# First two gate and up pairs, and the second feed-forward's entry unit, with both parts of x in one matmul

## The reference, cut to what matters

```python
x = x + rms_norm(mix, norm_mix_post[l])
h2 = rms_norm(x, norm_ffn_pre[l])
ff = jnp.einsum('bsf,fd->bsd',
                jax.nn.silu(jnp.einsum('bsd,df->bsf', h2, w_gate[l]))
                * jnp.einsum('bsd,df->bsf', h2, w_up[l]), w_down[l])
...
# second block: h = rms_norm(x); relu(h @ w_ff1) ** 2 @ w_ff2; 4096 hidden channels
```

## Time and profile before

| what | value |
|---|---|
| median of three runs | 805.6 us |
| span of the profiled execution | 804.3 us |
| PE busy | 798.1 us, 99%, 5838 matmuls |
| PEld busy | 700.9 us, 87% |
| DVE busy | 570.7 us, 71% |
| ACT busy | 465.5 us, 58% |
| POOL busy | 108.7 us, 14% |
| weight loads by SP | 49.8% of 16 DMA engines' span |

### The profile page before, as it was taken

One profiled execution on the slowest core, in us unless ns is written; L12 is line 12 of the kernel. 1 busy time (PEld: TensorE's weight loads), 2 busy tenths in 40 slices (PEclk: granted clock), 3 DMA queues, 4 the chain that ended last, 5 costly groups with the idle time before them and its releaser, 6 DMA issues.

```text
span 804.3 us, 13652 instructions
## 1 busy us (share of the span) xinstructions
PE 798.1 (99%) x5838; PEld 700.9 (87%) x5838; DVE 570.7 (71%) x712; ACT 465.5 (58%) x614; POOL 108.7 (14%) x82
## 2 busy tenths in 40 slices
PE   9999999999999999999999999999999999999998
PEld 7999988788888898888888889987899888888886
DVE  5877996897576586766676688598978865556653
ACT  6679774665534575454454575477787644444442
POOL 0102790662000000000000010111610100000000
PEclk9999999999999999999999999999999999999999
DMA  9844444443653655554655555465323555555641
GB/s 312 296 168 158 159 158 158 152 165 113 214 169 146 222 189 172 206 187 180 210 174 192 208 167 203 165 211 167 129 90 109 202 179 187 209 173 194 202 165 52
DMA packets 37820, 143.03 MB, mean 178 GB/s; under 512 B 9426, under 2 KB 11490, under 8 KB 24320
## 3 DMA queue, kind: packets, MB, share of 16 engines
q1 hardware_dynamic: 36576, 138.69, 49.8%
q0 software_dynamic: 1040, 3.43, 1.2%
q10 hardware_dynamic: 144, 0.04, 0.0%
HBM read 141.08 MB, written 1.06 MB: 177 GB/s over the span
## 4 chain that ended last, share of the span: by engine, by line
PE 93%; DMA 3%; DVE 2%; ACT 1%; issue 0%; POOL 0%; SPq 0%; POOLq 0%
PE ps L2380 8%; PE ps L2373 7%; PE ps L2025 6%; PE ps L2274 6%; PE ps L2272 6%; PE ps L2273 6%; PE ps L1957 6%; PE ps L2031 6%; PE ps L2028 6%; PE ps L1958 6%; PE ps L1959 6%; PE ps L2378 4%; PE ps L2375 4%; PE ps L2133 2%; DMA raw<-w 1%; DMA x<-xT 1%
## 5 line engine op out<-in xcount | busy, mean ns | idle before, releaser
L1178 DVE TENSOR_TENSOR wlo<-raw,whi 128x2048 fp32r<-128x2048 f32 (+2 forms) x128 | 289.4, 2263 | 73.9 <-ACT whi L622 72.5
L622 ACT ACTIVATE whi<-raw 128x2048 fp32r<-128x2048 f32 (+2 forms) x128 | 241.3, 1887 | 105.7 <-DMA raw<-w 105.6
L1957 PE MATMUL ps<-xx,whi 128*128 128x256 f32 x396 | 114.2, 288 | 0.0
L1958 PE MATMUL ps<-xx,whi 128*128 128x256 f32 x396 | 112.0, 283 | 0.0
L1959 PE MATMUL ps<-xx,wlo 128*128 128x256 f32 x396 | 112.0, 283 | 0.0
L2272 PE MATMUL ps<-whi,xx 128*128 128x512 f32 x216 | 84.1, 389 | 0.0
L2273 PE MATMUL ps<-whi,xx 128*128 128x512 f32 x216 | 84.0, 389 | 0.0
L2274 PE MATMUL ps<-wlo,xx 128*128 128x512 f32 x216 | 84.0, 389 | 0.0
L2025 PE MATMUL ps<-whi,xx 128*128 128x512 f32 x208 | 83.0, 399 | 0.0
L2031 PE MATMUL ps<-wlo,xx 128*128 128x512 f32 x208 | 81.1, 390 | 0.0
L2028 PE MATMUL ps<-whi,xx 128*128 128x512 f32 x208 | 81.0, 390 | 0.0
(11 more groups left out here) (322 smaller groups left out, 1366.7 us busy)
## 6 DMA issues: line engine op xcount, KB each, us to landing
raw<-w SPq DMA_DIRECT2D x105, 1024.0 KB, 4.8
raw<-w SPq DMA_DIRECT2D x42, 512.0 KB, 4.8
raw<-w SPq DMA_DIRECT2D x8, 256.0 KB, 6.3
x<-xT SPq DMA_DIRECT2D x4, 256.0 KB, 5.7
work<-bias_scratch POOLq DMA_DIRECT2D x1, 1024.0 KB, 7.2
raw<-w SPq DMA_DIRECT2D x4, 192.0 KB, 3.2
out<-x SPq DMA_DIRECT2D x3, 256.0 KB, 2.5
raw<-w SPq DMA_DIRECT2D x3, 240.0 KB, 3.3
```

What stands on the lines that cost most here:

```text
L622: A(hi, full, ACT.Copy).then_inc(sem("hi_ready"), 1)
L1178: V.tensor_tensor(lo, full, hi.bitcast(F32), ALU.subtract)\
L1957: mm(out, hi, xh[:, tile, :], start=start, stop=False, skip_group_check=skip)
L1958: mm(out, hi, xl[:, tile, :], start=False, stop=False, skip_group_check=skip)
```

## The change

- Pairs 0 and 1 of the first feed-forward and the entry pair of the second go to the wide form. Their banks are `ENTRY_BANKS`: unit 43 in 6 and 1, unit 44 in 0 and 2, gate 1 in 3 and 4, up 1 in 1 and 7; unit 99 in 5 and 6.
- `first_wide` replaces `first_unit` for units 43 and 99. Its first pair of input tiles stays at 256 columns; for the other three the high weight meets `xx` in one matmul, which comes after the wait for `act_lo`.
- `wide_tiles` gets a hook `low`, used by unit 44 to wait for its low weights behind the first 8 matmuls.
- ACT's order gets the low copies of units 43 and 44 ahead of the splits of units 46 and 47, and of the later entry units; the ReLU of the second entry pair goes.
- DVE's order is written anew: `gate_added(0)`, the split of 46, one add of up 0, `norm_factors`, the other add, the split of 47, and only then the wait for `bcs`.
- PE waits for `ple_copy` ahead of gate 1 (it was ahead of down 0), for `bcs` copied inside up 1, and for `gate_r` 2 ahead of down 0.

```diff
-WIDE1 = range(2, PAIRS1)
-WIDE2 = range(1, PAIRS2)
+WIDE1 = range(PAIRS1)
+WIDE2 = range(PAIRS2)
 GATE_BANKS, UP_BANKS = (0, 1), (2, 7)
+ENTRY_BANKS = ((6, 1), (0, 2), (3, 4), (1, 7))
...
             # ACT
+            low_copy(U_F1, 0, lows[0])
+            low_copy(U_F1, 1, lows[0])
             split_hi(U_F1 + RING)
+            low_copy(U_F1 + 1, 0, lows[1])
+            low_copy(U_F1 + 1, 1, lows[1])
             split_hi(U_F1 + 1 + RING)
             bc_copy("n3")
             silu_pair(0)
             hidden_hi(0, "hid", 0, 0)
...
-            relu_pair(0, U_F2, 5)
+            low_copy(U_F2, 0, lows[0])
+            low_copy(U_F2, 1, lows[0])
...
             # DVE
+            gate_added(0, U_F1)
+            split_lo(U_F1 + RING)
+            up_added(U_F1 + 1, 0)
             norm_factors("n3", 1)
-            split_lo(U_F1 + RING)
+            up_added(U_F1 + 1, 1)
+            split_lo(U_F1 + 1 + RING)
             dve.wait_ge(sem("norm_bcs"), before("bcs", "n3") + 1)
-            gate_scaled(0, U_F1, U_F1 % RING)
-            split_lo(U_F1 + 1 + RING)
-            hidden(0, 0, U_F1 + 1, (U_F1 + 1) % RING)
+            gate_scaled()
+            silu_scaled(0)
+            hidden_wide(0, 0)
             hidden_lo(0, 0, "hid", 0)
             for j in range(1, PAIRS1):
+                gate_added(j, u)
+                gate_scaled()
                 split_lo(u + RING)
+                silu_scaled(j)
+                up_added(u + 1, 0)
                 if j < PAIRS1 - 1:
                     split_lo(u + 1 + RING)
+                up_added(u + 1, 1)
+                hidden_wide(j, j % 2)
...
-            relu_square(0, 0, 5)
+            square_wide(0, U_F2, 0)
             hidden_lo(0, 0, "hid2", 8)
...
             # PE
+            def first_wide(u, base, x_name):
+                arrived(u)
+                o = [ps[b] for b in WIDE[u][1]]
+                for pair in range(4):
+                    blocks = [(m, k) for k in (2 * pair, 2 * pair + 1) for m in range(2)]
+                    w = lambda m, k: slice((8 * m + k) * P, (8 * m + k + 1) * P)
+                    pe.wait_ge(sem("act_hi"), before("hi", x_name) + pair + 1)
+                    for m, k in blocks:
+                        mm(o[m][:, 0:T], wlo[:, u % SLOTS, w(m, k)], xh[:, base + k, :], start=k == 0, ...)
+                        if pair == 0:
+                            mm(o[m][:, 0:T], whi[:, u % SLOTS, w(m, k)], xh[:, base + k, :], ...)
+                    pe.wait_ge(sem("act_lo"), before("lo", x_name) + pair + 1)
+                    for m, k in blocks:
+                        high = whi[:, u % SLOTS, w(m, k)]
+                        if pair == 0:
+                            mm(o[m][:, T:2 * T], high, xl[:, base + k, :], ...)
+                            continue
+                        last = mm(o[m][:, :], high, xx[:, base + k, :, :], ...)
...
-            first_unit(U_F1, 8, "n3")
-            first_parts(U_F1 + 1, 8)
+            first_wide(U_F1, 8, "n3")
+            pe.wait_ge(sem("hi_ready"), U_F1 + 2)
+            used(wide_tiles(U_F1 + 1, 8, low=lambda: arrived(U_F1 + 1)))
             norm_stats("n3", sq3)
...
                 first = j == 1
                 pe.wait_ge(sem("lo_ready"), u + 1)
+                if first:
+                    pe.wait_ge(sem("ple_copy"), PLE_EARLY // 2)
+                else:
                     pe.wait_ge(sem("gate_r"), j)
                     pe.wait_ge(sem("hid_y"), j)
+                used(wide_tiles(u, 8, between=(lambda: norm_bc("n3")) if first else None))
                 pe.wait_ge(sem("lo_ready"), u + 2)
+                if first:
                     pe.wait_ge(sem("gate_r"), 1)
+                used(wide_tiles(u + 1, 8, between=factors_read if first else None))
                 pe.wait_ge(sem("lo_ready"), u + 3)
                 pe.wait_ge(sem("hid_lo"), j)
                 if first:
-                    pe.wait_ge(sem("ple_copy"), PLE_EARLY // 2)
+                    pe.wait_ge(sem("gate_r"), 2)
...
-            first_unit(U_F2, 0, "n6", 5)
+            first_wide(U_F2, 0, "n6")
```

More of the change, by code:

```diff
@@ L160, with gate_unit @@
 TURNED = dict(mo=(1, 2, 0, 7), ff=(3, 7, 0, 4))
+def gate_unit(j):
+    return U_F1 + 3 * j - 1 if j else U_F1
 def wide_units():
@@ L167, in wide_units @@
     for j in WIDE1:
-        units += [(U_F1 + 3 * j - 1, GATE_BANKS), (U_F1 + 3 * j, UP_BANKS)]
+        u = gate_unit(j)
+        gate, up = ENTRY_BANKS[2 * j:2 * j + 2] if j < 2 else (GATE_BANKS, UP_BANKS)
+        units += [(u, gate), (u + 1, up)]
     for j in WIDE2:
-        units.append((U_F2 + 2 * j - 1, (UP_BANKS, GATE_BANKS)[j % 2]))
+        units.append((U_F2 + 2 * j - 1, (UP_BANKS, GATE_BANKS)[j % 2]) if j else (U_F2, (5, 6)))
     return {u: (i, banks) for i, (u, banks) in enumerate(units)}
@@ L876, in _ @@
             for j in range(1, PAIRS1):
[L877 to L880, removed]
+                u = gate_unit(j)
+                low_copy(u, 0, lows[0])
                 split_hi(u + RING)
-                if wide:
-                    low_copy(u, 1, lows[0])
-                    low_copy(u + 1, 0, lows[1])
+                low_copy(u, 1, lows[0])
+                low_copy(u + 1, 0, lows[1])
                 silu_pair(j)
@@ L887, in _ @@
                     split_hi(u + 1 + RING)
-                if wide:
-                    low_copy(u + 1, 1, lows[1])
+                low_copy(u + 1, 1, lows[1])
                 hidden_hi(j, "hid", 2 * (j % 2), j % 2)
@@ L1504, in _ @@
             ahead(U_PLE)
[L1507 to L1524, removed]
             def low_added(u, m, out, low):
@@ L1530, in low_added, with gate_added, gate_scaled, silu_scaled @@
                 return V.tensor_tensor(out[:, m, :], ps[banks[m]][:, 0:T], low[:, m, :], ALU.add)
-            def gate_wide(j, u):
-                dve.wait_ge(sem("gated"), j)
+            def gate_added(j, u):
+                if j:
+                    dve.wait_ge(sem("gated"), j)
                 count(low_added(u, 0, two(silu), lows[0]))
                 link(low_added(u, 1, two(silu), lows[0]))
+            def gate_scaled():
                 V.tensor_tensor(two(silu), two(silu), factors_by_tile(2), ALU.mult).then_inc(sem("gate_r"), 1)
-            def up_wide(j, u, m):
-                if m == 0:
-                    dve.wait_ge(sem("silu"), j + 1)
+            def silu_scaled(j):
+                dve.wait_ge(sem("silu"), j + 1)
+                if j:
                     dve.wait_ge(sem("hid_y"), j)
-                    V.tensor_tensor(two(gated), two(silu), factors_by_tile(2), ALU.mult).then_inc(sem("gated"), 1)
+                V.tensor_tensor(two(gated), two(silu), factors_by_tile(2), ALU.mult).then_inc(sem("gated"), 1)
+            def up_added(u, m):
                 count(low_added(u, m, lows[1], lows[1]))
@@ L1550, in hidden_wide @@
                 dve.wait_ge(sem("dve_chain"), chained[0])
-                dve.wait_ge(sem("hid_lo"), j)
+                if j:
+                    dve.wait_ge(sem("hid_lo"), j)
                 V.tensor_tensor(hid[slot_h], two(gated), lows[1], ALU.mult).then_inc(sem("hid_y"), 1)
@@ L1907, in _ @@
             ahead(U_WO + 3)
[L1910 to L1915, removed]
             def square_wide(j, u, slot_h):
-                dve.wait_ge(sem("hid2_y"), j)
+                if j:
+                    dve.wait_ge(sem("hid2_y"), j)
                 count(low_added(u, 0, two(silu), lows[j % 2]))
                 link(low_added(u, 1, two(silu), lows[j % 2]))
-                dve.wait_ge(sem("hid2_lo"), j)
+                if j:
+                    dve.wait_ge(sem("hid2_lo"), j)
                 V.scalar_tensor_tensor(hid[slot_h], two(silu), 0.0, two(silu), ALU.max, ALU.mult).then_inc(sem("hid2_y"), 1)
-            relu_square(0, 0, 5)
+            square_wide(0, U_F2, 0)
             hidden_lo(0, 0, "hid2", 8)
@@ L2351, in _, with wide_tiles @@
             used(ple_part(range(4, PLE_EARLY)))
[L2354 to L2363, removed]
+            def first_wide(u, base, x_name):
[6 more added lines that the diff above has]
+                    for m, k in blocks:
+                        mm(o[m][:, 0:T], wlo[:, u % SLOTS, w(m, k)], xh[:, base + k, :], start=k == 0, stop=False, skip_group_check=True)
+                        if pair == 0:
+                            mm(o[m][:, 0:T], whi[:, u % SLOTS, w(m, k)], xh[:, base + k, :], start=False, stop=False, skip_group_check=True)
+                    pe.wait_ge(sem("act_lo"), before("lo", x_name) + pair + 1)
+                    for m, k in blocks:
+                        high = whi[:, u % SLOTS, w(m, k)]
+                        if pair == 0:
+                            mm(o[m][:, T:2 * T], high, xl[:, base + k, :], start=False, stop=False, skip_group_check=True)
+                            continue
+                        last = mm(o[m][:, :], high, xx[:, base + k, :, :], start=False, stop=k == 7, skip_group_check=True)
+                        if (m, k) == (0, 7):
```

(14 more changed lines are left out.)

22 lines of the change are left out of this document (1 added, 21 removed).

## The result

Five runs of each gave 808.79 us (808.6 to 809.22) for the changed kernel and 805.53 us (804.92 to 805.84) for the one before: 3.26 us more, a ratio of 1.0041 with a 95% interval of 1.003 to 1.0052. The prediction was 808.7 us.

A forecast was written before the change was run, and what follows sets the result against it. PE was taken as the bound (93% of the chain). Span 804.3 + 2.8 (first feed-forward) + 0.25 (second) = 807.35 us; with 1.3 from span to median, 808.65, given as 808.7; range 806.4 to 810.4.

The forecast's parts named there:

- all four waits: First feed-forward, PE standing before the transposes (1.33 us), up 1 (0.15), down 0 (0.85) and gate 2 (0.95): 3.28 us.
- the backlog was not longer: Rival: hand-overs in the four chains each take 0.1 us more, giving 1.5 us more, 810.2 us; chance 6%.
- The signs: Expected PE gaps: over 1 us before transposes, 0.1 to 0.3 up 1, 0.6 to 1.1 down 0, 0.7 to 1.2 gate 2.
- The entry units: First feed-forward's entry unit +0.20 us, paid for by 0.21 won in up 0; second feed-forward's entry unit +0.20 us.
- a wait's reaction: PE's delay in reacting to a new wait: 0 to 0.2 us possible, taken as 0.05.
- stall 1: PE at gate 1's transposes, waiting for rx, ready at 295.85 while PE arrives at 294.54: 1.33 us.
- the work put ahead of the norm factors: DVE queue before eps and rx: adds for gate 0, split of unit 46, one up 0 add; rival text said 3.8 us.
- the first or the third: PE stalls before gate 1's transposes (1.33 us, for rx) and before down 0 (0.85 us, for gate 1's scaling).
- The 0.0134 us per merged matmul: PE saving per weight block when two 256-column matmuls become one of 512; 72 merged blocks give 0.96 us.
- the waits don't bite: Rival, placed at gate 1's transposes: only PE's 0.96 us saving counts, 804.6 us, not slower; chance 8%.
- only the first ones count: Rival: stalls before the transposes and up 1 remain, those before down 0 and gate 2 do not; 806.5 us, chance 12%.
- The clock: Rival: PE's clock falls after a stall; one 5.57 us unit running twice as long would give 814 us; chance 2%.

The follow-up runs named there:

- e_nf: Changed kernel, with DVE making the norm factors ahead of the weight split of unit 46 instead of behind it: 809.2 us.
- e_down: Changed kernel, with down 0 adding first to banks 5 and 6 and waiting for gate 1's scaling only before banks 3 and 4: 809.64 us.
- e_hy: Changed kernel, with gate 2 waiting for pair 1's product between its two output tiles instead of at its start: 807.97 us.
- e_act: Changed kernel, with both low copies of gate 1 on ACT ahead of the weight split of unit 48: 807.94 us.
- e_best: Changed kernel with DVE, ACT, down 0 and gate 2 waits reordered and both entry units narrow: 805.2 us beside 805.79 before, ratio 0.9992.
- e_order: Changed kernel, with norm factors ahead of the split of unit 46 and gate 0's scaling ahead of that of unit 47: 808.45 us.

## Why the prediction was right

**Direction and place.** DVE's backlog, not PE's work, decided, and all four waits stood where they were put. Three are listed with the releaser that was named; the one before up 1 is seen in its step alone, and gate 0's scaling, made from 297.52 to 298.20, ends 0.15 us before up 1 starts. Gate 2 was forecast 2.78 us late and was 2.77.

**The stalls, start to start.** Before the transposes 0.99 us (forecast 1.33), up 1 0.20 (0.15), down 0 0.74 (0.85), gate 2 1.02 (0.95). The sum is 2.95 against 3.28, so the backlog was not longer than forecast. The signs were written as gaps, and as gaps two fell short: 0.83 before the transposes, where "over 1 us" stood, and 0.48 before down 0, where 0.6 to 1.1 stood.

**The entry units were the weak term.** The first took 6.66 us instead of 6.29, +0.37 where I had +0.20, and up 0 gave back 0.17 (5.68 to the sums against 5.85) instead of 0.21. So gate 1 started 0.21 late instead of level. The second took +0.32 instead of +0.20. The reason is in the rows: four wide matmuls behind a wait take 1.04 us (281.06 to 282.10), and 0.93 without one (284.39 to 285.32); I had 0.91. So the step behind a wait was some 0.11 longer, and I had priced a wait's reaction at 0.05 in all. The same 0.2 us made stall 1 shorter, since PE came later to it while DVE did not: rx was forecast for 295.85 and came at 295.82, the entry unit's earlier start of 0.75 added. That is why gate 2 held, although two terms of the sum were off.

**The total.** The two stages together were forecast at 3.05 us and took 3.17. That the total lies 0.1 us from the forecast is in part luck: the five runs of the changed kernel spread over 0.6 us. The 1.3 us between span and median is no constant either; where a run's time and span are both on record they mostly lie 1.8 apart (808.6 and 806.8). One figure of the rivals was also off: the work put ahead of the norm factors is 3.3 us by the prediction's own steps (0.33 + 0.46 + 2.2 + 0.33), not 3.8. No time was worked out from it.

**The wait that takes over.** The prediction adds up four stalls. That is right for the sum, but e_nf and e_down show that a stall is no price of its wait: taken away alone, the first or the third gives nothing (49.28, 49.10). e_hy, which hides the last wait, and e_act, which shortens the chain, give 1.01 and 1.05.

**The 0.0134 us per merged matmul** came out as 0.0104 in e_best. By the 2.5 ns that the Trainium skill, page "TensorE: Matmul & The Clock Gate", section "Wait — 56ns, not 53.3ns?", states, its 48 would have saved an estimated 0.12 us. The trace shows 0.50.

**Rivals.** That the waits don't bite, and that only the first ones count, are refuted by the changed kernel's rows. The clock stayed at its upper level, 2.4 GHz, through all the waits, of which the longest shown is the 1.49 us of e_down. These are windows of the changed kernel over the two stretches (length; busy time and count of PE, PEld, DVE, ACT, POOL; then the granted clock, 1.00; DMA share and GB/s):

```profile
278.60:311.20 32.60, 30.13 (x177) 24.67 (x176) 28.39 (x39) 22.75 (x33) 0.70 (x1) 1.00 0.48 170
623.40:640.80 17.40, 17.23 (x94) 14.49 (x93) 13.86 (x22) 10.33 (x15) 0.00 (x0) 1.00 0.61 217
```

## What to carry to other kernels

When an engine with 71% average load gets a few hundred nanoseconds of new work, look at what stands in its queue at that place. Here what counted was what stood behind a weight split of 2.3 us on DVE (the norm factors and gate 0's scaling, 0.60 us in e_order) or of 1.8 us on ACT (one copy, 1.05 us in e_act). Place the value that a busy engine waits for ahead of the long background work, on every queue of its chain; mending one wait can merely move the stall to the next one, as in e_nf and e_down. And sum the prize first: 72 matmuls of fixed cost were worth under 1 us, less than the place of one copy.

## What the runs showed that I had not expected

A wait is worth more than the idle time that the profile lists: the one listed as 0.75 us gave back 1.01 (e_hy). Part of it is that the first matmul step behind a wait is about 0.1 us longer (1.04 against 0.93 us for four wide matmuls). Whether the wait itself lengthens the step is not shown: gate 1, which follows the norm's small sums without a listed wait, has the same step of 1.95 us for eight wide matmuls (291.24 to 293.19), where up 2 takes 1.81 (316.77 to 318.58).

And the loop of before has pair products with only about 0.4 us to spare (pair 2's ends at 324.57 + 0.69 in the profile before, gate 3 starts at 325.67). From gate 3 to gate 4 the kernel before takes 16.57 us, and so does the changed one. In seven of the other eleven profiles, all of kernels whose loop is the old one, it takes 0.18 to 0.73 us more, 0.73 in e_hy and 0.65 in e_down. Where I followed the wait back (e_hy, e_down, e_all) it began with a weight transfer that came late; why it came late is open.
